# An opening RMS norm done in token rows instead of in feature rows, with the first input blocks loaded ahead of the parameters

## What is computed

```python
def rms_norm(x, g):
    xf = x.astype(jnp.float32)
    y = xf * lax.rsqrt(jnp.mean(xf * xf, axis=-1, keepdims=True) + RMS_EPS)
    return (y * g.astype(jnp.float32)).astype(x.dtype)

# first_block, layer 0:  h = x
u = rms_norm(h, norm_mix[0])
zxbcdt = u @ in_proj                 # 1024 -> 6176: z, x/B/C, dt
z, xbc, dt = jnp.split(zxbcdt, ...)
xbc = jax.nn.silu(causal_dwconv(xbc, conv_w, conv_b))
```

## Time and profile before

| | |
|---|---|
| median of 3 executions | 2794.19 us (2794.03 to 2797.14) |
| the profiled execution | 2802.82 us, span 2801.1 us |
| PE busy | 2684.8 us (96%) |
| DVE busy | 1993.4 us (71%) |
| ACT busy | 1392.8 us (50%) |
| POOL busy | 235.4 us (8%) |
| HBM | 416.33 MB read, 42.43 MB written |
| mean granted clock of TensorE | 0.990 |

### The profile page before, as it was taken

One profiled execution on the slowest core, in us unless ns is written; L12 is line 12 of the kernel. 1 busy time (PEld: TensorE's weight loads), 2 busy tenths in 40 slices (PEclk: granted clock), 3 DMA queues, 4 the chain that ended last, 5 costly groups with the idle time before them and its releaser, 6 DMA issues.

```text
span 2801.1 us, 36390 instructions
## 1 busy us (share of the span) xinstructions
PE 2684.8 (96%) x12549; PEld 2058.3 (73%) x12549; DVE 1993.4 (71%) x3046; ACT 1392.8 (50%) x2137; POOL 235.4 (8%) x209
## 2 busy tenths in 40 slices
PE   8999999999999999999999989999999999999996
PEld 7877877888887877888876756686567777777762
DVE  4788754777637976777538556464569999999986
ACT  4767552222325554223323333444458877777772
POOL 0000000000000000000004400000012322222210
PEclk9999999999999999999999999999999999999998
DMA  3222213232232132332333561322459999999996
GB/s 111 73 60 68 91 62 108 87 104 90 79 87 90 61 35 66 105 100 81 83 118 112 129 114 57 110 91 95 166 206 357 337 341 347 351 344 341 343 348 269
DMA packets 317200, 435.12 MB, mean 155 GB/s; under 512 B 45339, under 2 KB 199011, under 8 KB 316835
## 3 DMA queue, kind: packets, MB, share of 16 engines
q1 hardware_dynamic: 299299, 395.61, 43.6%
q0 software_dynamic: 17792, 38.06, 4.5%
HBM read 416.33 MB, written 42.43 MB: 164 GB/s over the span
## 4 chain that ended last, share of the span: by engine, by line
PE 68%; SPq 17%; DVE 7%; issue 3%; ACT 3%; DMA 3%; DVEq 0%; ACTq 0%
PE tp L1289 40%; SPq L953 12%; SPq L960 4%; PE tp L1245 4%; PE tp L1337 2%; PE tp L1396 2%; PE tp L1398 2%; PE tp L1397 1%; PE tp L1800 1%; PE tp L1983 1%; PE tp L1984 1%; PE tp L1985 1%; DMA wring<-ytab 1%; PE mp L1591 1%; PE mp L1590 1%
## 5 line engine op out<-in xcount | busy, mean ns | idle before, releaser
L1289 PE MATMUL tp<-sq_r,arena_r 128*128 128x512 f32 x1056 | 422.9, 400 | 3.5 <-DVE uT_r L2814 3.5
L1289 PE MATMUL tp<-sq_r,wring_r 128*128 128x512 f32 x1056 | 420.1, 398 | 0.0
L1289 PE MATMUL tp<-uT_r,arena_r 128*128 128x512 f32 x1056 | 416.4, 394 | 0.0
L1289 PEld LDWEIGHTS tp<-sq_r,arena_r 128*128 128x128 f32 x1056 | 199.0, 188 | 53.3 <-issue 5.8
L1289 PEld LDWEIGHTS tp<-uT_r,arena_r 128*128 128x128 f32 x1056 | 199.2, 189 | 49.6 <-issue 1.4
L1289 PEld LDWEIGHTS tp<-sq_r,wring_r 128*128 128x128 f32 x1056 | 199.2, 189 | 48.9
L2786 DVE TENSOR_TENSOR wring_r<-wring,arena_r 128x2048 fp32r<-128x2048 f32 x82 | 187.1, 2321 | 56.5 <-ACT arena_r L2111 56.4
L1289 PE MATMUL tp<-arena_r,wring_r 128*128 128x512 f32 x564 | 223.1, 396 | 0.0
L2359 ACT ACTIVATE arena<-arena 128x512 f32<-128x512 f32 x44 | 27.8, 633 | 299.9 <-DVE arena L2872 299.8
L2111 ACT ACTIVATE arena_r<-wring 128x2048 fp32r<-128x2048 f32 x82 | 152.4, 1906 | 43.4 <-DVE arena L2976 11.8
L3676 DVE TENSOR_TENSOR arena_r<-arena,arena_r 128x1024 fp32r<-128x1024 f32 x128 | 150.5, 1217 | 0.5 <-ACT arena_r L2699 0.5
(11 more groups left out here) (581 smaller groups left out, 6201.0 us busy)
## 6 DMA issues: line engine op xcount, KB each, us to landing
arena<-in_w_exp_down SPq DMA_DIRECT2D x64, 1024.0 KB, 16.6
wring<-in_w_exp_gu SPq DMA_DIRECT2D x64, 768.0 KB, 10.2
uT<-in_w_exp_gu SPq DMA_DIRECT2D x32, 768.0 KB
sq<-in_w_exp_gu SPq DMA_DIRECT2D x32, 768.0 KB, 10.5
wring<-in_f_up_w SPq DMA_DIRECT2D x22, 1024.0 KB, 5.2
wring<-in_f_up_w SPq DMA_DIRECT2D x44, 512.0 KB, 6.7
wring<-in_w_exp_gu SPq DMA_DIRECT2D x32, 512.0 KB, 16.9
wring<-in_f_down_w SPq DMA_DIRECT2D x32, 448.0 KB, 5.8
```

The source lines that it names most:

```text
L1289: ins = nc.tensor.matmul(b[:], parts[wp][:, kk, m * P:(m + 1) * P], xparts[xp][:, kk, :], start=n_k == 0 and q == 0, stop=n_k == k - 1 and ...
```

## The change

- SP loads `norm_mix` first, then the four x blocks, then the twelve weight loads of group 0, and only then the other parameters. The small loads behind them keep their order.
- VectorE takes for each block of 128 tokens the mean and variance of its rows (two `bn_stats` of 512, one `bn_aggr`), forms the mean square as mean^2 + variance, and after ScalarE's root the reciprocal and a diagonal matrix with 1/rms of the block's tokens.
- TensorE turns the x blocks to `hT` as before, and then multiplies each block of x by its diagonal, which turns and normalizes it at once: 32 products of 128 x 128 by 128 x 128 into all eight PSUM banks (`tp` and `mp`), one bank for each block of 128 features.
- The weights of the norm are turned alone, into 8 columns (`mix_gain`). ScalarE evicts each bank with them as scale to `u_hi`; VectorE forms `u_lo` from the bank and `u_hi`. Projection 0 waits for the first four low parts.
- Gone are the squares, the products by ones, the 128 x 512 reciprocal, the normalized copy `uT`, and the 26 products of `keep_clock`.
- The other parameters are turned on TensorE after projection 0 and taken by ScalarE after the four evictions of projection 0 (their tiles now stand behind the four of projection 0 in the count that guards the banks).

```diff
@@ SP @@
+            b, r0, n, src = par.rows[0]
+            sp.dma_start(pk[r0:r0 + n, b, :], src).then_inc(row_in[0], 16)
             for c in range(TC):
                 sp.dma_start(xtok[:, c, :], A["x"][0][c * P:(c + 1) * P, :]).then_inc(row_in[c], 16)
-            for b, r0, n, src in par.rows:
-                sp.dma_start(pk[r0:r0 + n, b, :], src).then_inc(param_in, 16)
             for q in range(4):
                 quarter_in(0, q)
+            for b, r0, n, src in par.rows[1:]:
+                sp.dma_start(pk[r0:r0 + n, b, :], src).then_inc(param_in, 16)
@@ TensorE @@
+            pe.wait_ge(row_in[0], 16 * 2)
+            nc.tensor.transpose(mp[0][:, 0:NK], pk[0:NK, 0, :], ident[0:NK, 0:NK]).then_inc(stat_ready, 1)
+            for c in range(TC):
+                if c:
                     pe.wait_ge(row_in[c], 16)
+                for h in range(2):
+                    turn([xtok[:, c, k * P:(k + 1) * P] for k in range(4 * h, 4 * h + 4)])
+            pe.wait_ge(sq_ready, NK - TC)
+            first, second = range(NBANK), range(NBANK, NK)
+            for c, ks in ((0, second), (1, second), (0, first), (1, first), (2, range(NK)), (3, range(NK))):
+                if ks is first and c == 0:
+                    pe.wait_ge(tile_evac, 2 * TC)
+                pe.wait_ge(un_ready, DIAG_STEP[c])
+                for k in ks:
+                    ins = nc.tensor.matmul(MIX_BANKS[k][:, c * P:(c + 1) * P], xtok[:, c, k * P:(k + 1) * P], diag[:, c, :],
+                                           start=True, stop=True)
+                    if c == TC - 1:
+                        ins.then_inc(stat_ready, 1)
-            keep_clock(26)
...
+            pe.wait_ge(xlo_ready, NBANK)
             project(0, {}, fresh=True)
             nx.inc(NK)
+            pe.wait_ge(param_in, 16 * (len(par.rows) - 1))
+            for b in range(0, NPB, 4):
+                turn([pk[0:min(P, par.n - bb * P), bb, :] for bb in range(b, min(b + 4, NPB))])
             pe.wait_ge(wdt_split, 2)
@@ ScalarE @@
+            for k in range(NK):
+                act.wait_ge(sq_ready, NK)
+                act.wait_ge(stat_ready, 1 + k + 1)
+                nc.scalar.activation(u_hi[1][:, k, :], MIX_BANKS[k][:], ACT.Copy, scale=mix_gain[:, k:k + 1]).then_inc(xhi_ready, 1)
+                if k in (1, 3, 5):
+                    group_hi(0, ((k + 1) // 2,))
             act.wait_ge(misc_in, 16 * 5)
             nc.scalar.activation(wdt_hi[1], wdt, ACT.Copy).then_inc(wdt_split, 1)
             act.nop().then_inc(silu_ready, NBANK)
             group_hi(1, (0, 1, 2))
             for q in range(4):
                 take_conv(0, q)
-            first_taps(0)
+            for b in range(0, NPB, 4):
+                n = min(4 * P, par.n - b * P)
+                take(pcol[:, b * P:b * P + n], n=n)
+            first_taps(0, NPB_TILES)
@@ VectorE @@
+            def token_square(c):
+                dve.wait_ge(row_in[c], 16 if c else 32)
+                for half in range(2):
+                    ins = V.bn_stats(tok_stats[:, 2 * c + half, :], xtok[:, c, 512 * half:512 * half + 512])
+                link(ins)
+                link(V.bn_aggr(tok_mv[:, c, :], tok_stats[:, 2 * c:2 * c + 2, :]))
+                V.scalar_tensor_tensor(tok_ms[:, c:c + 1], tok_mv[:, c, 0:1], tok_mv[:, c, 0:1], tok_mv[:, c, 1:2], ALU.mult, ALU.add)\
+                 .then_inc(un_ready, 1)
+            def token_diagonal(c):
+                dve.wait_ge(sq_ready, NK - TC + c + 1)
+                link(V.reciprocal(tok_rs[:, c:c + 1], tok_rs[:, c:c + 1]))
+                V.tensor_scalar(diag[:, c, :], ident[:], tok_rs[:, c:c + 1], None, ALU.mult).then_inc(un_ready, 1)
```

More of the change, by code:

```diff
@@ L238, in build @@
         mp = [ctx.enter_context(nc.psum_tensor(f"mp{i}", [P, T], F32)) for i in range(4)]
+        MIX_BANKS = tp + mp
+        MS_STEP, DIAG_STEP = (1, 2, 4, 6), (3, 5, 7, 8)
         w_ready = [sem(f"w_ready{r}") for r in range(NSLOT)]
@@ L270, in build @@
         xtok = carve(TC, D)
+        diag = carve(TC, P)
+        tok_stats = carve(2 * TC, 6)
+        tok_mv = carve(TC, 2)
+        tok_ms, tok_rs = carve(TC + 1), carve(TC)
+        mix_gain = carve(NK)
+        assert par.rows[0][0:2] == (0, 0) and par.base["norm_mix"] == 0
         top[0] = 0
@@ L643, in build @@
                  "s5_x": 18, "s5_yd": 16, "s5_yev": 32,
-                 "tok_out": 16 * 7, "y_out": 16 * 5, "uc_in": 16 * len(par.rows)}
+                 "tok_out": 16 * 7, "y_out": 16 * 5, "uc_in": 16 * (len(par.rows) - 1)}
         y_out, uc_in = misc_in, param_in
@@ L1460, in _ @@
             pe.wait_ge(consts_ready, 1)
-            for c in range(TC + 1):
-                if c < TC:
+            pe.wait_ge(row_in[0], 16 * 2)
+            nc.tensor.transpose(mp[0][:, 0:NK], pk[0:NK, 0, :], ident[0:NK, 0:NK]).then_inc(stat_ready, 1)
+            for c in range(TC):
+                if c:
                     pe.wait_ge(row_in[c], 16)
[L1464 to L1475, removed]
+                for h in range(2):
[11 more added lines that the diff above has]
+                        ins.then_inc(stat_ready, 1)
             nsq.inc(NK)
-            nstat.inc()
-            keep_clock(26)
+            nstat.inc(1 + NK)
             def turn_dt():
@@ L2074, in _ @@
             for c in range(TC):
-                pe.wait_ge(row_in[c], 16 * 3)
+                pe.wait_ge(row_in[c], 16 * (3 if c else 4))
                 add_rank(c, rank_rows[6])
@@ L2196, in take_conv, with first_taps @@
                 nconv.inc()
-            def first_taps(g):
+            def first_taps(g, since=0):
                 act.wait_ge(tile_evac, tiles.v)
@@ L2203, in first_taps @@
                     c = 2 * g + q if q < 2 else (16 + g if q == 2 else 24 + g)
-                    nc.scalar.activation(acc[q], raw[(tiles.s + q) % NBANK][:, PAD:PAD + T], ACT.Identity,
+                    nc.scalar.activation(acc[q], raw[(tiles.s - since + q) % NBANK][:, PAD:PAD + T], ACT.Identity,
                                          scale=pc("a_conv_w", 96 + c), bias=pc("a_conv_b", c)).then_inc(tap_in, 1)
@@ L2250, in _, with token_root @@
             act.wait_ge(consts_ready, 1)
+            nc.scalar.activation(tok_ms[:, TC:TC + 1], kc[:, 1:2], ACT.Sqrt)
+            act.wait_ge(stat_ready, 1)
+            nc.scalar.activation(mix_gain, mp[0][:, 0:NK], ACT.Copy).then_inc(sq_ready, NK - TC)
+            def token_root(c):
+                act.wait_ge(un_ready, MS_STEP[c])
+                nc.scalar.activation(tok_rs[:, c:c + 1], tok_ms[:, c:c + 1], ACT.Sqrt, bias=kc[:, 0:1]).then_inc(sq_ready, 1)
             for c in range(TC):
@@ L2254, in _ @@
                     take(hT[:, 4 * h:4 * h + 4, s])
[L2255 to L2269, removed]
+                token_root(c)
+            group_hi(0, (0,))
+            act.nop().then_inc(std_ready, 1)
+            nsq.inc(NK)
+            nstat.inc(1 + NK)
+            for k in range(NK):
[4 more added lines that the diff above has]
+                    group_hi(0, ((k + 1) // 2,))
             act.wait_ge(misc_in, 16 * 5)
@@ L2985, in _ @@
             dve.nop().then_inc(conv_ready, NBANK)
-            tiles.inc(NPB_TILES + NK)
+            tiles.inc(NK)
             dve.wait_ge(consts_ready, 1)
@@ L2989, in _ @@
                 V.tensor_copy(pick2[r:r + HEADS, :], ident[r:r + HEADS, r:r + HEADS])
-            nstat.inc()
+            def token_square(c):
[10 more added lines that the diff above has]
+                V.tensor_scalar(diag[:, c, :], ident[:], tok_rs[:, c:c + 1], None, ALU.mult).then_inc(un_ready, 1)
+            for c in range(TC):
+                token_square(c)
+                if c >= 1:
+                    token_diagonal(c - 1)
+            token_diagonal(TC - 1)
+            group_lo(0, (0,))
+            nstat.inc(1 + NK)
             dve.wait_ge(std_ready, nstd.v + 1)
             nstd.inc()
[L2993 to L3002, removed]
+            for k in range(NK):
+                dve.wait_ge(xhi_ready, k + 1)
+                V.scalar_tensor_tensor(u_lo[1][:, k, :], MIX_BANKS[k][:], mix_gain[:, k:k + 1], u_hi[1][:, k, :].bitcast(F32),
+                                       ALU.mult, ALU.subtract).then_inc(xlo_ready, 1)
+                nx.inc()
+                if k in (3, 5, 7):
+                    group_lo(0, ((k - 1) // 2,))
             dve.wait_ge(wdt_split, 1)
@@ L3007, in _ @@
             conv_pair(0, (2, 3))
+            tiles.inc(NPB_TILES)
             nstat.inc()
```

## The result

The changed kernel took 2807.07 us in the median of seven runs (2803.89 to 2811.83), the kernel before 2797.94 us in the median of seven (2794.03 to 2801.73). The ratio is 1.0028, 95% interval 1.0017 to 1.0038: about 7.8 us slower (the two medians by themselves lie 9.1 us apart). The profiled execution of the changed kernel took 2807.07 us.

The account below looks back on a forecast made before the run. Bounds taken: the norm up to 28.5 us, then loads after 45 us, with `a_d_skip` releasing ScalarE at 47.6. Sum: 4.7 + 1.1 + 2.1 - 1.4 + 2.6 = +9.1 us on 2794.19, so 2803.3 us; range 2797.5 to 2807.

Parts of the forecast that it names:

- Opening: Norm and projection 0 on TensorE: projection 0 runs from 21.8 to 43.7 us, 7.0 us won at this point.
- a release that the norm does not move: ScalarE, before evicting projection 0: waits for the `a_d_skip` loads until 47.6 us, a time set by SP's queue.
- The bank wait: TensorE after projection 0: parameter turns wait for ScalarE's first eviction until 55.4 us, +4.7 us.
- Turns and clock: TensorE after projection 0: eight exposed parameter turns, +1.1 us, and a clock slowed by idleness, +2.1 us.
- Absorbed: Between projection 1 and the first SSD group's opening: existing slack takes up 1.4 us of the delay.
- SP's line: SP's DMA queue: weight loads moved ahead of the parameters delay the issue of `a_d_skip`, +2.6 us.
- "queue not blocked" rival: SP's DMA queue: its line moves by -1.1 to +0.5 us, total +5.4 to +7.0 us; chance 0.20.
- the signs that hung on it: Changed profile: `a_d_skip` issued at 27 to 28 us, landing near 50, TensorE idle 12 to 14, group near 93.5.
- Carried to the end: After the first group's opening: the whole sum of +9.1 us stays to the kernel's end.

Follow-up runs that it names:

- experiment 1: The changed kernel with `a_d_skip` loaded as one contiguous row and picked apart by two VectorE copies; 2796.61 us against 2799.02 for the kernel before, ratio 0.999.
- experiment 5: The changed kernel with all other parameters again loaded ahead of group 0's weights on SP; ratio 1.0015 to the kernel before.
- experiment 6: The kernel before with a third `a_d_skip` load of the same form, into a spare place and waited for; slower by 0.32% than the kernel before.
- Experiment 4: The changed kernel with 48 products by the identity in TensorE's gap after projection 0; ratio 1.0019 to the kernel before.
- experiment 8: The kernel before, unchanged, profiled a second time; dt products at 50.43 us, first SSD group opening at 82.88 us.
- experiment 3: The changed kernel with the parameters turned into the banks `mp[2]` and `mp[3]`; ratio 1.0008 to the kernel before.

## Why the prediction was right, and which term was not

Forecast 2803.3 us for a median of 2794.19, +9.1 us or 0.33%; measured 0.28% (0.17 to 0.38), some 7.8 us. In seven runs the kernel before has a median of 2797.94 us, 3.8 us above the one that the forecast was added to, so the changed kernel's own median of 2807.07 lies at the upper end of the stated range, 2797.5 to 2807; against the kernel before, the forecast is off by 1.3 us. The mechanism is the one forecast. The closeness of the number is in part luck: at the group's opening, where the sum was made, the profiles show 5.9 us instead of 9.1. Step by step:

- **Opening.** Forecast: projection 0 from 21.8 to 43.7 us. Measured 20.65 to 42.75 us. The turns were done sooner than I had counted; the products by the diagonal and the statistics cost what the rows of similar ones said (two statistics in 1.29 us).
- **The gain is lost at a release that the norm does not move.** Right, and shown by experiments 1, 5 and 6. The release came at 47.9 us, against 47.6 before.
- **The bank wait.** Forecast 4.7 us late on arrival (55.4 us) before SP's shift; measured 3.65 (54.31). I had taken the evictions' start of 54.75 us as fixed; it was 53.58. Asking for group 1's quarters earlier is not what brought that: the kernel before, with its quarters asked for at 34.3 us as ever, begins the evictions at 53.21 us in its second profile. The 54.75 was late in that one execution (its third quarter took 6.41 us to land, 4.88 in the changed kernel).
- **Turns and clock.** Forecast 1.1 + 2.1 us; measured 1.94 + 1.80 = 3.7 us with the slow clock in both: the turns took 1.94 us, and the dt products 7.38 instead of 5.58. Experiment 4 puts the clock at 2.1 to 2.6. (Read again, give 4.5 us at half rate, not 4.2: the clock is at 0.50 from 2755.03 us, and 0.87 in the mean of the last 2 us is 0.5 us more of it. The term would be 2.2 us.)
- **Absorbed.** Forecast 1.4 us, measured 7.4 at projection 1 less 5.9 at the opening: 1.5. But the second profile of the kernel before opens at 82.88 us, and against that one hardly anything is absorbed (0.2 us). The term was taken from a single execution in which ScalarE's line happened to be late, the same 1.5 us as at the evictions.
- **SP's line.** This is the term that was mis-sized: +2.6 us forecast, +0.77 us measured for the issue of `a_d_skip` (25.52 instead of 24.75), and +0.3 for its landing. The queue did block, as I had argued, but less: the twelve loads took 8.08 us to issue instead of 7.18, not the 9.5 to 11 of my estimate, and the small loads behind them were no slower. The "queue not blocked" rival was nearer at this step. Of the 2.6 us next to nothing reached TensorE's position. With it go the signs that hung on it: `a_d_skip` issued at 27 to 28 us (25.52), landing near 50 (47.9), a gap of 12 to 14 us (11.56), the group at 93.5 us (90.33).
- **Carried to the end.** That the whole sum is carried on is not shown step by step. At 361 us the changed kernel is 7.4 us behind the first profile of the kernel before and 8.9 behind the second; at the end of the spans it is 4.2 us behind the first (2805.3 against 2801.1) and 5.6 behind the second (2799.7), with the change of pace of experiment 8 in between. The runs say 7.8.

The rule of the Trainium skill (DMA: Bandwidth & Descriptors, "Why a DMA increments its semaphore by 16 and not by 1"), by which 64 partitions would be spread over 16 engines, was to make `a_d_skip` a matter of 0.7 us by the prediction's estimate. The runs go against that result: 9.9 us between the two landings in the changed kernel (26.2 + 21.7 = 47.9 less 25.5 + 12.5 = 38.0), and 9.9 us more for a third load in experiment 6 (56.6 less 46.7). They do not show how many engines took part. The advice of the Trainium skill on the same page ("Rules for kernel authors"), that a strided last dimension becomes a descriptor for each element and should be made contiguous, fits experiment 1: the same numbers as a contiguous row landed in 4.2 us.

## What to carry to other kernels

A saving ahead of a wait with a release time of its own is worth only the distance to that release, so read first who waits for what behind the stretch that you shorten, above all a small load at the end of a queue. Work that is moved out of a hidden place needs buffers whose owner is not queued behind such a wait. And a load of single elements is to be judged by its landing time, not by its bytes: 8 KB in single elements held a queue for some 20 us here, and a contiguous row with two small copies took its place. And one profile is one execution: two of the terms above were read from a start that a second profile of the same kernel puts 1.5 us earlier.

## What the runs showed of the hardware

- A load of 4 KB in elements of 4 bytes landed 9.9 to 10.1 us after the one of the same kind before it (changed kernel 9.9, experiment 6 9.9, kernel before 10.1), and DMAs behind them in the same queue wait: one issue stood for 7.9 us in the changed kernel (5.7 us in the earlier trace rows).
- TensorE's grant fell to 0.50 in or right behind idle gaps of 11.56 us (changed kernel), 7.43 (experiment 6), 6.71 and 4.53 (experiment 5), and of 2.8 us in two of four profiles: in experiments 1 and 3, not in the changed kernel and experiment 4. With eight products by the identity in that last gap it stayed at 1.00, in one profile. After a fall 3.4 us (experiment 1) to 6 us (experiment 3) of work ran at half rate.
- TensorE's pace in one and the same stage differed by 1% between executions (216 and 218 products in 50 us), over hundreds of microseconds, with the granted clock at 1.00 in all, in kernels whose code for that stage is the same. A single profile is no proof of a change of a few microseconds far from the edit.
